# The second attention layer's latent projections as seven block products, with other places for modulation passes, squares and weight sums

## The chip, the core and the metric

The kernel runs on one core of a Trainium2 chip. The core's engines are TensorE (PE; its weight loads are PEld), VectorE (DVE), ScalarE (ACT), GpSimd (POOL) and SyncE (SP), with 16 DMA engines. SBUF is the memory beside the engines, PSUM the banks that matrix products write. The metric is the device time of one execution in microseconds (us); 2938.09 is the median of three.

## The reference

All data are float32, the width D is 1024, and there are 512 latent and 256 context tokens. The time looked at here is the first of two blocks, two layers of attention:

```python
hx = rmsnorm(x, norm_w) * (1 + scale) + shift       # latent, 512 tokens
hc = rmsnorm(cx, norm_w) * (1 + scale_c) + shift_c  # context, 256 tokens
px, pc = split_cols(hx @ w_in), split_cols(hc @ w_in)   # q, k, v of A, B, C and gates
ya = global_gqa(...)           # A: 8 heads, 2 of k and v, q and k normed, rope
yb = neighbourhood_attn(...)   # B: 8 heads, relative bias, masked by place
yc = window_gqa(...)           # C: 8 heads, 2 of k and v, rope, band mask, sink
x = x + gate * (concat(ya, yb, yc) * silu(px[9])) @ w_out
```

In layer 0 the context's outputs are needed too, in layer 1 the latent ones alone. Modulation vectors of the second block (`silu(c) @ w_mod`), which need nothing of the attention, are also computed meanwhile. The second block (an RG-LRU and Hyena layer and a conformer, each with a mixture of experts) is not touched.

## The kernel before

**Pairs and steps.** Heads are worked in 12 pairs, `PAIRS`: four B, four A, four C. A pair has one step for each tile of 128 queries: 6 in layer 0 (768 tokens), 4 in layer 1 (512). `schedule` (L272) writes one order of items for a layer, and each engine's `attention` walks through it: `S` (scores of both heads into BIG, L1402 to L1413), `T` (transposes of the step before's probabilities, L1426, into PT, which ACT copies at L2156), `E` (exponentials, ACT L2145), a filler, and `O` (outputs, PE L1442, read by DVE at L2613). DVE adds biases (L2707) or masks (L2718), takes the maximum (L2723), and after the exponentials scales by the reciprocal sum (L2604, L2606). The `T` of a step stands behind the `S` of the next.

**Projections.** The filler of a pair's steps is the next pair's projections: one unit of weights (1024 x 256) for keys and values (`kv`; one for each B pair, one for all A, one for all C) and one for queries and gates (`qg`, each pair). In layer 0 they go by blocks: the unit and the tokens are cut into 2 x 2 blocks, and `BLOCK_PRODUCTS`, seven products in the order 1, 2, 6, 5, 7, 3, 4, take the place of eight, each of `BLOCK_K` = 4 matmuls of 128 x 128 by 384 tokens into one of the two PJ banks (L1097 is the helper that issues every matmul). ACT copies products 1, 6, 5 and 4 out of PSUM (L2091), DVE adds 2, 7 and 3 to them (L2560). For it DVE makes four sums of token blocks once (`block_tokens`, into `BLOCK_TOKENS` in XC) and POOL four sums of weight blocks a unit (`add_weights`, L1031 to L1036), one of them in place in the weight ring W. `block_slots` (L168) deals the items out over the steps by `weight`.

In layer 1 each of k, v, q and g is a plain product (`through`: 8 matmuls over K of 512 latent columns, and of 256 context columns for k and v). A and C pairs get their values by token tiles (`vt`: 48 matmuls of 128 columns, copied by DVE, `values` L2694). Then come, in A pairs, the `norm_` items (squares by ACT L2177, L2178, sums by PE L1354, ACT L2125, L2129), in A and C pairs the `rope_` items (PE L1364, DVE L2584 to L2588). In B pairs and in layer 0 `v_tokens` (L1345) transposes the values. Gates go through a tanh (ACT L2102) and a product on DVE.

**Modulation.** 168 passes over rows of 1024 weights on DVE (L2462, each with a read of its accumulator) stand in the order as `mod` items. `plan_modulation` (L90) gives each step a room (`MODS_ROOM`), none in C heads and none in the last step but one from the last B pair on; `schedule` puts the first 1 (layer 0's B heads) or 2 of a step ahead of `E`, and `with_modulation` the others between fillers. POOL loads the rows into a ring of five places (`mod_place`, L1001): the next load waits for the passes of the row five before.

**POOL's queue** is one list, sorted by place in the order: row loads, biases (L991), weight sums, reloads. The sums of a unit wait for product 3 (the sixth) of the unit before. Behind the list POOL reloads the context (L1064, after h was scaled) and two weights of the second block (L1066, L1067).

Of the kernel before, what the change touches and what calls it, by code (L numbers as in the profile page):

```python
# [17 lines left out]
P = 128  # L18
# [68 lines left out]
MODS_ROOM = [{"B": 3.6, "A": 1.4, "C": 0.0}, {"B": 2.6, "A": 2.6, "C": 0.0}]  # L87


def plan_modulation():  # L90


    out, room = [], 0.0
    pause = 0
    for layer in range(DEPTH):
        tiles = STEPS[layer] // len(PAIRS)
        for n in range(STEPS[layer]):
            i, t = divmod(n, tiles)
            at = n + (STEPS[0] if layer else 0)
            ropes = t == tiles - 2 and i >= 3  # L100
            room += 0.0 if ropes else MODS_ROOM[layer][PAIRS[i][0]]
# [8 lines left out]
    assert all(at < 8 * 6 or STEPS[0] <= at < STEPS[0] + 8 * TT for at in out)  # L110
    return out


MOD_STEPS = plan_modulation()
MODS_SECOND = MOD_STEPS[MODS_FIRST - 1] + 1

# [19 lines left out]
BLOCK_N = NA // 2  # L136
# [7 lines left out]
def inserted_by_blocks(i):  # L144
# [6 lines left out]
    elif kind == "B":  # L151
        out += by_blocks(i, "kv")
    elif kind == "A" and j == 0:
        out += by_blocks(i, "kv", 0, 6) + [("square", i, "k")] + by_blocks(i, "kv", 6) + [("norm_k", i)]
    elif j == 0:
        out += by_blocks(i, "kv")
# [11 lines left out]
def block_slots(i, tiles):  # L168


    todo = inserted_by_blocks(i)
    early = BLOCK_K if PAIRS[i - 1][0] != "B" else 0
    room = tiles if PAIRS[i][0] == "B" else tiles - 1
    total, done, least, before = sum(weight(x) for x in todo[early:]), 0, 0, 0
    out = [(-1, item) for item in todo[:early]]
    for item in todo[early:]:
        at = max(min(int(done * room / total), room - 1), least)
        done += weight(item)
# [8 lines left out]
def inserted(layer, i):  # L187


    if layer == 0:  # L190
        return inserted_by_blocks(i)
    kind, j = PAIRS[i]
    parts = 2 if layer == 0 else 1

    def through(what, parts):
        return [("mm", i, what, part, k) for part in range(parts) for k in range(KT)]

    def by_tokens(tiles):
        return [("vt", i, t, k) for t in tiles for k in range(KT)]

    if kind == "B":
        out = through("k", 2) + through("q", parts) + through("v", 2)
        gates = through("g", parts)
        return out + gates[:BLOCK_K] + [("v_tokens", i)] + gates[BLOCK_K:]
    if j == 0:
        out = through("k", 2) + through("q", parts)
        if kind == "A":
            out.append(("norm_k", i))
        out += by_tokens(range(4)) + by_tokens(range(4, 6))
        if kind == "A":  # L210
            out.append(("norm_q", i))
        return out + [("rope_k", i)] + through("g", parts) + [("rope_q", i)]
    gates = through("g", parts)
    out = through("q", parts)
    if kind == "C":
        return out + [("rope_q", i)] + gates
    if parts == 2:
        return out + gates[:KT] + [("norm_q", i)] + gates[KT:] + [("rope_q", i)]
    return out + [("norm_q", i)] + gates + [("rope_q", i)]


def weight(item):
# [4 lines left out]
    return {"block": 1.5, "square": 0, "tanh": 0, "gate": 0, "next": 0, "vt": 0.5, "v_tokens": 2.5, "norm_k": 3, "norm_q": 3, "rope_k": 2, "rope_q": 2}[what]  # L227
# [9 lines left out]
def filler(item):  # L237
# [3 lines left out]
    return item[0] == "vt" or item[0] == "block" and item[4] < BLOCK_K - 1  # L241


def begins_unit(item):

    if item[0] == "mm":
        return item[2] in ("k", "q") and item[3:] == (0, 0)
# [24 lines left out]
def schedule(layer):  # L272
# [6 lines left out]
    for i in range(1, len(PAIRS)):  # L279
        if layer == 0:  # L280
            for at, item in block_slots(i, tiles):
                slots[(i - 1) * tiles - 1 + at].append(item)
            continue
        todo = inserted(layer, i)
        total, done, least, before = sum(weight(x) for x in todo), 0, 0, None
        for item in todo:
            at = min(int(done * tiles / total), tiles - 1)
            done += weight(item)
            if item[0].startswith(("norm_", "rope_")):

                least = min(at + (before is not None and before >= at), tiles - 1)
            at = max(at, least)
            before = at
            slots[(i - 1) * tiles - 1 + at].append(item)
    tail = 1 + max(n for n in slots if any(item[0] in ("mm", "vt", "block") for item in slots[n]))
# [5 lines left out]
    for n in range(-1, last + 1):  # L301
        if n + 1 <= last:
            order.append(("S", n + 1))
        if n >= 0:
# [3 lines left out]
            early = 1 if layer == 0 and steps[n][0] < 4 else 2  # L308
# [116 lines left out]
def build(nc, A):  # L425
# [15 lines left out]
    with ExitStack() as ctx:  # L441
# [79 lines left out]
        def mod_place(row):  # L521

            x = row % MOD_RING
# [117 lines left out]
        def sem(name):  # L641
# [103 lines left out]
        BLOCK_TOKENS = XC[:, :, :].rearrange("p a b -> p (a b)")\  # L745
            .rearrange("p (x k n) -> p x k n", x=4, n=BLOCK_N)
        ADDED = ARENA_AND_RS[:, ROPE_AT + N:ROPE_AT + N + 3 * BLOCK_K * P]\
            .rearrange("p (x k n) -> p x k n", x=3, n=P)

        def block_uses():  # L750
# [3 lines left out]
            for y, item in enumerate(schedule(0)[1]):  # L754
# [10 lines left out]
                elif what.startswith("norm_"):  # L765
                    me.next_pj()
                    me.next_pj()
# [4 lines left out]
        def block_parts(i, which, dst, src, half):  # L772


            a = half * BLOCK_N
            if PAIRS[i][0] != "B" or which == "g":
                return [(dst[:, a:a + BLOCK_N], src[:, 0:BLOCK_N])]
            rows = BLOCK_N // GRID_W
            grid = dst[:, 0:N].rearrange("p (c r) -> p c r", r=ROWS)
            if half == 0:  # L780
                return [(grid[:, :, 0:rows], by_columns(src[:, 0:BLOCK_N]))]
            n = N - BLOCK_N
            return [(grid[:, :, rows:ROWS], by_columns(src[:, 0:n])), (dst[:, N:NA], src[:, n:BLOCK_N])]
# [97 lines left out]
        def row_place(x):  # L881
# [3 lines left out]
            freed = -1 if x < MOD_RING else max(place["mod", y] for y, (row, _) in enumerate(MOD_OPS) if row == x - MOD_RING)  # L885
            second = x % MOD_RING >= 2 and min(steps) >= STEPS[0]
# [97 lines left out]
        def _(pool):  # L984
# [9 lines left out]
            def load_mod_rows(x):  # L994


                if x >= MOD_RING:
                    pool.wait_ge(mod_made, ROW_DONE[x - MOD_RING])
                if row_place(x)[1]:
                    pool.wait_ge(products_filled, len(LATE))  # L1000
                pool.dma_start(mod_place(x), A["mod_rows"][x]).then_inc(mod_loaded[x % MOD_RING], 16)  # L1001
# [12 lines left out]
            first_block_unit = first_units.index(("w_in", 0, 1))  # L1014

            def weights_of(u):

                n = first_block_unit + u
# [3 lines left out]
            def add_weights(u):  # L1022
# [4 lines left out]
                if u:  # L1027
                    pool.wait_ge(pj_filled, uses[u - 1][5][0])
                else:
                    pool.wait_ge(h_scaled, 2 * KT)  # L1030
# [3 lines left out]
                pool.tensor_tensor(a21, a21, a11, ALU.add).then_inc(weights_added, 1)  # L1034
# [12 lines left out]
            for u in range(len(uses)):  # L1047
                jobs.append((uses[u - 1][5][1] if u else -1, 3, u))
            jobs.append((uses[-1][6][1], 4, 0))
            for _, what, x in sorted(jobs):  # L1050
                if what == 3:
                    add_weights(x)
                elif what == 4:
                    pool.wait_ge(pj_filled, uses[-1][6][0])
# [8 lines left out]
            pool.wait_ge(h_scaled, 4 * KT)  # L1063
# [2294 lines left out]
```

## Time and profile before

| | us |
|---|---|
| median of the runs (2937.65 to 2938.37) | 2938.09 |
| the profiled execution | 2939.53 |
| its span | 2937.7 |
| PE busy in the span | 2817.2 (96%) |
| DVE busy | 1363.4 (46%) |
| ACT busy | 770.1 (26%) |
| POOL busy | 225.2 (8%) |

Layer 0's attention takes the span's 44 to 669 us (B heads to 339, A heads to 536), its output products follow to 771, and layer 1's attention runs from 779 to 1289 (B heads to 1020, A heads to 1186, C heads to 1289; the filler, which is one pair ahead, changes its kind about one pair earlier). The rest, to 2938, is the second block. A busy share over the whole span says little of a stage; the windows and waits below do.

### The profile page before, as it was taken

To read this page: it belongs to the slowest core of one execution; us is meant where nothing else is said; L and a number is where in the kernel's file an instruction comes from. 1 tells how busy PE (TensorE), PEld (TensorE's weight loads), DVE (VectorE), ACT (ScalarE), POOL (GpSimd) and SP (SyncE) were. 2 spreads that over 40 slices of the span, in tenths; PEclk is the share of its full clock that TensorE was granted. 3 is DMA by queue.
4 is the path that set the end of the run, shared out by engine and by line. 5 is a ranking of instruction groups with operands and counts; after the bars stand their busy time and mean duration, and the time that the engine had idled before them with its cause. 6 is when DMAs were issued, how large, how long until landed. Compare 5 with 4: busy or idle time off the path is not lost.

```text
span 2937.7 us, 33851 instructions
## 1 busy us (share of the span) xinstructions
PE 2817.2 (96%) x13312; PEld 1523.4 (52%) x13312; DVE 1363.4 (46%) x2569; ACT 770.1 (26%) x1410; POOL 225.2 (8%) x253
## 2 busy tenths in 40 slices
PE   7999899999999999999999989999999999999998
PEld 3555555655555655576444644444445734444442
DVE  2696776775355674674485741111115813121112
ACT  3334454441222453433251120000003232000001
POOL 2233212100011010000000000000002300000000
PEclk9999999999999999999999999999999999999999
DMA  8244222111145443112110158999993217999996
GB/s 315 90 162 153 91 73 87 37 73 58 79 155 169 135 152 106 44 46 89 63 61 20 56 216 359 421 421 422 421 420 145 107 67 299 410 421 422 421 421 282
DMA packets 90673, 586.60 MB, mean 200 GB/s; under 512 B 10192, under 2 KB 10192, under 8 KB 29232
## 3 DMA queue, kind: packets, MB, share of 16 engines
q1 hardware_dynamic: 69696, 502.56, 42.6%
q0 software_dynamic: 20848, 82.26, 8.4%
q8 instruction: 89, 1.46, 0.2%
q14 instruction: 40, 0.33, 0.0%
HBM read 582.68 MB, written 2.10 MB: 199 GB/s over the span
## 4 chain that ended last, share of the span: by engine, by line
PE 68%; DVE 6%; ACT 2%; issue 1%; DVEq 0%; ACTq 0%
PE BIG L1097 43%; PE PJ L1097 11%; PE BIG L1941 4%; PE PT L1426 2%; PE PT L1442 2%; DVE ARENA L2984 1%; PE PT L1097 1%; PE BIG L1409 1%; PE PJ L1146 1%; PE BIG L1413 1%; PE PT L1917 1%; DVE ARENA L3036 0%; DVE ARENA L3035 0%; ACT ARENA L2145 0%; PE BIG L1402 0%
## 5 line engine op out<-in xcount | busy, mean ns | idle before, releaser
L1097 PE MATMUL BIG<-ARENA 128*64 128x512 f32 (+3 forms) x2720 | 565.4, 458 | 6.5 <-DVE ARENA L3058 2.5
L1097 PEld LDWEIGHTS BIG<-ARENA 128*64 128x64 f32 (+1 forms) x2720 | 302.2, 169 | 255.4 <-issue 224.3
L1097 PE MATMUL PJ<-HT,W 128*128 128x512 f32 (+2 forms) x1040 | 400.3, 533 | 7.3 <-DVE ARENA L2694 2.6
L1097 PE MATMUL BIG<-W,ARENA 128*64 128x512 f32 (+1 forms) x1280 | 282.0, 573 | 0.9 <-DVE ARENA L2906 0.9
L1097 PEld LDWEIGHTS PJ<-HT,W 128*128 128x128 f32 x1040 | 193.8, 193 | 166.3 <-issue 127.9
L3087 DVE SCALAR_TENSOR_TENSOR XC<-BIG,MOD,XC 128x512 f32<-128x512 f32 x128 | 90.2, 747 | 379.4 <-PE BIG L1941 379.4
L2156 ACT ACTIVATE ARENA<-PT 128x512 f32<-128x512 f32 (+1 forms) x264 | 145.1, 583 | 416.8 <-PE PT L1426 416.5
L1097 PE MATMUL BIG<-HT,W 128*128 128x512 f32 (+1 forms) x600 | 236.6, 553 | 2.4 <-DVE ARENA L2860 2.1
L1097 PEld LDWEIGHTS BIG<-W,ARENA 128*64 128x64 f32 (+1 forms) x1280 | 107.4, 142 | 161.0 <-issue 154.9
L2723 DVE TENSOR_REDUCE STAT<-BIG 128x1 f32<-128x512 f32 (+5 forms) x240 | 169.9, 724 | 39.2 <-PE BIG L1413 34.2
L1097 PE MATMUL BIG<-HT,ARENA 128*64 128x512 f32 (+1 forms) x632 | 182.9, 573 | 0.0
L1097 PEld LDWEIGHTS BIG<-HT,W 128*128 128x128 f32 x600 | 114.3, 191 | 120.5 <-issue 111.7
L2145 ACT ACTIVATE ARENA<-BIG,STAT 128x512 f32<-128x512 f32 (+5 forms) x240 | 170.6, 717 | 22.3 <-DVE STAT L2723 21.3
L1426 PE MATMUL PT<-CONST,ARENA 128*128 128x128 f32 x1024 | 150.7, 282 | 22.0 <-DVE ARENA L2613 14.5
L1426 PEld LDWEIGHTS PT<-CONST,ARENA 128*128 128x128 f32 x1024 | 111.5, 141 | 82.8 <-issue 60.8
L1442 PEld LDWEIGHTS PT<-ARENA 128*64 128x64 f32 x2048 | 110.3, 136 | 68.9 <-issue 63.9
L2462 DVE CUSTOM_DVE_ANT_0 SPILL<-ARENA,W,VEC 128x1024 bf16<-128x1024 f32 x100 | 139.1, 1391 | 4.3
L1442 PE MATMUL PT<-ARENA 128*64 128x128 f32 x2048 | 139.3, 278 | 1.4 <-ACT ARENA L2156 1.4
L1097 PE MATMUL BIG<-ARENA,W 128*128 128x512 f32 (+2 forms) x400 | 136.2, 494 | 0.1
L2606 DVE TENSOR_SCALAR ARENA<-ARENA,STAT 128x512 f32<-128x512 f32 (+3 forms) x240 | 128.3, 535 | 8.5
L1941 PE MATMUL BIG<-ARENA 128*128 128x512 f32 x256 | 115.0, 602 | 0.0
L3077 DVE TENSOR_TENSOR ARENA<-ARENA,BIG 128x1024 f32<-128x1024 f32 x16 | 19.5, 1221 | 204.2 <-PE BIG L1097 204.2
(325 smaller groups left out, 3068.4 us busy)
## 6 DMA issues: line engine op xcount, KB each, us to landing
ARENA<-in_exp_w SPq DMA_DIRECT2D x168, 1024.0 KB, 18.1
W<-in_exp_w SPq DMA_DIRECT2D x144, 1024.0 KB, 16.7
W<-in_units SPq DMA_DIRECT2D x89, 1024.0 KB, 4.9
HT<-in_exp_w SPq DMA_DIRECT2D x72, 1024.0 KB, 21.9
ARENA<-in_mod_rows POOLq DMA_DIRECT2D x76, 512.0 KB, 4.5
W<-in_mod_rows POOLq DMA_DIRECT2D x52, 512.0 KB, 4.5
ARENA<-in_bias_b POOLq DMA_DIRECT2D x16, 384.0 KB, 4.9
XC<-in_x SPq DMA_DIRECT2D x1, 3072.0 KB, 10.1
```

Source lines behind the costliest of these rows:

```text
L1097: ins = pe.matmul(out, lhsT, rhs, start=start, stop=stop, skip_group_check=skip)
L1146: last = pe.matmul(PJ[0][:, 0:512], const("ident"), CONST[:, 0:512], start=True, stop=True)
L1409: pe.matmul(BIG[h][:, N - (b - a) * P:N], Q[rows, i % 2, t * P:t * P + P], keys[rows, a * P:b * P], start=True, stop=True)
L1426: last = pe.transpose(PT[:, a:a + P], PROB[:, h, y * P:y * P + P], const("ident"))
L1442: last = pe.matmul(PT[head * HD:head * HD + HD, bank * 512:bank * 512 + P], V[:, buf_of[i], tile, head * HD:head * HD + HD], PTS[:, at:at ...
L1941: last = pe.matmul(BIG[k_use % 2][:, half * N:half * N + N], YK[:, m * P:m * P + P], GSCAT[:, :], start=True, stop=True)
L2145: act.activation(PROB[:, h, 0:b - a], BIG[h][:, a:b], ACT.Exp, bias=STAT[:, c:c + 1], accum_out=STAT[:, 4 + c:5 + c]).then_inc(probs_exp, 1)
L2156: act.activation(PTS[:, a:a + w], PT[:, bank:bank + w], ACT.Copy).then_inc(t_copied, 1)
L2462: dve.tensor_tensor_reduce(SPILL[:, :], mod_place(row), MODV[:, which, :], 1.0, vec("mod_b", at), ALU.mult, ALU.add, MOD[:, at:at + 1]).th ...
L2606: dve.tensor_scalar(probs, probs, STAT[:, 8 + c:9 + c], None, ALU.mult)\
L2723: dve.tensor_reduce(STAT[:, c:c + 1], out[:, a:b], AX.X, ALU.max, negate=True).then_inc(max_ready, 1)
L3087: ins = dve.scalar_tensor_tensor(XC[:, m, 0:N], BIG[k_use % 2][:, half * N:half * N + N], mod(group, 5, m, 0), XC[:, m, 0:N], ALU.mult, AL ...
```

## The change

- In layer 1 the latent part of `qg` of all pairs and of `kv` of all but the first pair goes by blocks too: 7 products of 4 matmuls by 256 columns. Context columns of k and v stay plain products. `vt` and `values` go; A and C values are transposed by `v_tokens`. DVE makes four token sums at the start of the layer, in parts of XC and U that hold nothing else then; POOL sums weights for 17 more units, one sum now in `THIRD_SUMS` in Q beside the latent columns.
- `block_slots` deals out both layers: a `square` goes one step behind the item before it (at most to the last step of the room), a `norm_` not before it; ropes stand in the last step of the filler, ahead of the first block product of the pair behind it (before, in A pairs, behind the last gate columns, in C pairs behind the queries).
- `modulation_room` gives the passes: 62, 27 and 17 in layer 0's B, A and C heads (before 71, 27 and 0), and 62 in layer 1, 12 of them in its C heads (before 70 and none). One pass of a step (before two, in layer 1) stands ahead of `E` in B heads. Rows whose passes lie in C heads use only two places of the ring (`plan_row_places`).
- `ADDED_AHEAD` sorts a unit's weight sums 16 items earlier in POOL's list.
- The reload of the context waits for layer 1's last block product.

```diff
-MODS_ROOM = [{"B": 3.6, "A": 1.4, "C": 0.0}, {"B": 2.6, "A": 2.6, "C": 0.0}]
+MODS_ROOM = [{"B": 2.9, "A": 1.4, "C": 0.7}, {"B": 2.3, "A": 1.4, "C": 0.8}]
+MODS_ROOM_OF = {("B", 0): 1.8, ("B", 1): 3.0, ("B", 2): 2.6, ("B", 3): 3.2, ("B", 4): 3.8, ("B", 5): 3.0}
+MODS_NONE = [(0, 3, 4), (0, 4, 0), (1, 3, 2), (1, 4, 0)]
+def modulation_room(layer, i, t):
+    kind = PAIRS[i][0]
+    if layer == 0 and (kind, t) in MODS_ROOM_OF:
+        return MODS_ROOM_OF[kind, t]
+    if t == STEPS[layer] // len(PAIRS) - 2 and kind == "A" or (layer, i, t) in MODS_NONE:
+        return 0.0
+    return MODS_ROOM[layer][kind]
...
+def plan_row_places():
...
+        at = min(range(2 if outputs else MOD_RING), key=lambda x: (last_of[x], x))
...
-BLOCK_N = NA // 2
+BLOCK_TOKENS_OF = [NA, N]
+BLOCK_NS = [n // 2 for n in BLOCK_TOKENS_OF]
...
+    elif kind == "B" or j == 0:
         out += by_blocks(i, "kv")
+        if layer:
+            context = [[("mm", i, what, 1, k) for k in range(KT)] for what in ("k", "v")]
+            squares = [("square", i, "k")] if kind == "A" else []
+            out += context[0] + squares + context[1] + ([("norm_k", i)] if kind == "A" else [])
...
+        if item[0] == "square":
+            squared = min(before + 1, room - 1)
+            out.append((squared, item))
+            continue
+        if item[0].startswith("norm_"):
+            at = least = max(at, squared)
...
-            early = 1 if layer == 0 and steps[n][0] < 4 else 2
+            early = 1 if steps[n][0] < 4 else 2
...
+        def third_sum(w, layer, k):
+            return THIRD_SUMS[:, k // 2, k % 2, :] if layer else w[:, k, P:2 * P]
...
+            ADDED_AHEAD = 16
...
-                jobs.append((uses[u - 1][5][1] if u else -1, 3, u))
+                jobs.append((uses[u - 1][5][1] - ADDED_AHEAD if u % BLOCK_UNITS else layer_starts[u // BLOCK_UNITS] - 1, 3, u))
...
-            pool.wait_ge(h_scaled, 4 * KT)
+            pool.wait_ge(pj_filled, uses[-1][6][0])
             pool.dma_start(XC[:, :, N:NA], A["ctx2"]).then_inc(ctx2_loaded, 16)
...
-            def block_tokens():
+            def block_tokens(layer):
+                dve.wait_ge(h_ready, (3 if layer else 2) * KT)
...
+                n = BLOCK_NS[layer]
```

## Rows read from the trace of the kernel before

**Rows 1.** Windows of five stretches: start:end, length, busy PE, PEld, DVE, ACT, POOL; clock.

```profile
44.00:300.00 256.00, 243.12 (x1174) 147.88 (x1174) 194.09 (x369) 95.77 (x212) 85.43 (x90) 0.98 0.44 150
300.00:669.00 369.00, 348.89 (x2137) 214.95 (x2138) 261.79 (x595) 173.66 (x378) 56.48 (x56) 0.99 0.21 68
779.00:979.00 200.00, 200.00 (x910) 115.60 (x910) 101.85 (x210) 60.44 (x135) 20.99 (x39) 1.00 0.43 147
979.00:1186.00 207.00, 193.72 (x1218) 120.22 (x1216) 130.87 (x243) 87.70 (x165) 17.21 (x31) 0.99 0.37 123
1186.00:1289.00 103.00, 100.86 (x675) 62.52 (x674) 75.08 (x200) 48.15 (x107) 0.00 (x0) 1.00 0.09 31
```

**Rows 2.** Waits of PE, 44 to 669 us: total us, times, longest.

```profile
PE PT L1426 <- DVE ARENA L2613: 14.5, 11, 3.2
PE PT L1426 <- ACT ARENA L2156: 6.1, 12, 1.3
```

**Rows 3.** Waits of PE, 779 to 1230 us.

```profile
PE BIG L1409 <- DVE ARENA L2588: 7.9, 5, 1.8
```

**Rows 4.** Windows of 10 us with a low clock, columns as in group 1.

```profile
115.00:125.00 10.00, 7.54 (x32) 4.97 (x29) 9.68 (x18) 3.95 (x9) 3.91 (x5) 0.83 0.81 267
1162.00:1172.00 10.00, 7.44 (x14) 2.98 (x13) 3.79 (x8) 1.97 (x5) 0.00 (x0) 0.83 0.32 105
```

**Rows 5.** Chain of work, 779 to 1230 us: start, us, what.

```profile
779.72 30.94 PE PJ L1097 x88
811.43 3.44 PE PJ L1097 x8
...
984.18 10.98 PE PJ L1097 x96
```

**Rows 6.** Timeline of DVE, 784 to 816 us: start, us, what, idle before.

```profile
815.53 0.69 DVE L2536 SCALAR_TENSOR_TENSOR ARENA<-ARENA,PJ 128x512 f32<-128x512 f32 x1 [29.62 <-ACT ARENA L2052]
```

**Rows 7.** Timelines of PE, DVE and ACT, a B step of layer 1.

```profile
872.75 0.70 PE L1402 MATMUL BIG<-ARENA 64*128 64x256 f32 x4
...
874.75 9.19 PE L1097 MATMUL PJ<-HT,W 128*128 128x256 f32 x24
...
873.92 0.43 DVE L2707 TENSOR_TENSOR BIG<-BIG,ARENA 128x256 f32<-128x256 f32 x1 [0.67 <-PE BIG L1413]
...
876.06 1.27 DVE L2462 CUSTOM_DVE_ANT_0 SPILL<-ARENA,W,VEC 128x1024 bf16<-128x1024 f32 x1
...
879.48 0.49 DVE L2606 TENSOR_SCALAR ARENA<-ARENA,STAT 128x512 f32<-128x512 f32 x1
...
876.76 0.19 ACT L2145 ACTIVATION_READ_ACCUMULATOR ARENA<-BIG,STAT 128x1 f32 x1
```

**Rows 8.** Timelines of PE and ACT, an A step of layer 1.

```profile
1054.82 1.13 PE L1409 MATMUL BIG<-ARENA 64*128 64x512 f32 x4
...
1058.10 0.60 PE L1426 MATMUL PT<-CONST,ARENA 128*128 128x128 f32 x4
...
1060.89 0.21 ACT L2145 ACTIVATION_READ_ACCUMULATOR ARENA<-BIG,STAT 128x1 f32 x1
```

**Rows 9.** Window of one C pair of layer 1, columns as in group 1.

```profile
1214.50:1242.90 28.40, 28.40 (x176) 16.42 (x174) 19.38 (x53) 12.31 (x28) 0.00 (x0) 1.00 0.12 38
```

**Rows 10.** Instructions of line 2462: min/median/max ns, first and last start.

```profile
L2462 DVE DVE_READ_ACCUMULATOR2_ANT MOD<- x168: 75/83/86, 99.5 to 1148.6; 128x1 f32 x168
L2462 DVE CUSTOM_DVE_ANT_0 SPILL<-ARENA,W,VEC x100: 1274/1280/2171, 112.0 to 1147.4; 128x1024 bf16<-128x1024 f32 x100
```

**Rows 11.** Groups of POOL, 44 to 700 us: busy us, mean ns, idle before.

```profile
L1034 POOL TENSOR_TENSOR W<-W 128x512 f32<-128x512 f32 x17 | 29.3, 1721 | 0.0
...
L1031 POOL TENSOR_TENSOR ARENA<-W 128x512 f32<-128x512 f32 x17 | 22.7, 1334 | 133.9 <-PE PJ L1097 130.6 <-DVE HT L2488 3.2
```

**Rows 12.** Timelines of DVE and PE, layer 0, 230 to 235 us.

```profile
230.29 2.06 DVE L2462 CUSTOM_DVE_ANT_0 SPILL<-ARENA,W,VEC 128x1024 bf16<-128x1024 f32 x1
...
234.81 0.63 PE L1426 MATMUL PT<-CONST,ARENA 128*128 128x128 f32 x4 [2.45 <-DVE ARENA L2613]
```

More of the change, by code:

```diff
@@ L109, in plan_modulation @@
     assert len(out) == len(MOD_OPS) and out[MODS_DONE[1] - 1] < STEPS[0]
-    assert all(at < 8 * 6 or STEPS[0] <= at < STEPS[0] + 8 * TT for at in out)
     return out
 MOD_STEPS = plan_modulation()
+def plan_row_places():
+    last_of = [-1] * MOD_RING
+    places, before, uses = [], [], [0] * MOD_RING
+    counts = []
+    for row in range(len(MOD_ROWS)):
+        steps = [MOD_STEPS[y] for y, (x, _) in enumerate(MOD_OPS) if x == row]
+        outputs = any(8 * 6 <= at < STEPS[0] or at >= STEPS[0] + 8 * TT for at in steps)
+        at = min(range(2 if outputs else MOD_RING), key=lambda x: (last_of[x], x))
+        places.append(at)
+        before.append(last_of[at])
+        last_of[at] = row
+        uses[at] += 1
+        counts.append(uses[at])
+    return places, before, counts
+ROW_PLACE, ROW_BEFORE, ROW_COUNT = plan_row_places()
 MODS_SECOND = MOD_STEPS[MODS_FIRST - 1] + 1
@@ L165, in inserted_by_blocks, with block_slots @@
     return out + ropes + [("tanh", i), ("next", i), ("gate", i)]
-def block_slots(i, tiles):
-    todo = inserted_by_blocks(i)
+def block_slots(layer, i):
+    tiles = STEPS[layer] // len(PAIRS)
+    todo = inserted(layer, i)
     early = BLOCK_K if PAIRS[i - 1][0] != "B" else 0
     room = tiles if PAIRS[i][0] == "B" else tiles - 1
-    total, done, least, before = sum(weight(x) for x in todo[early:]), 0, 0, 0
+    squared, total, done, least, before = 0, sum(weight(layer, x) for x in todo[early:]), 0, 0, 0
     out = [(-1, item) for item in todo[:early]]
@@ L177, in block_slots @@
         at = max(min(int(done * room / total), room - 1), least)
-        done += weight(item)
+        done += weight(layer, item)
         if item[0] == "next":
@@ L184, in block_slots, with weight @@
     return out
[L187 to L222, printed above, removed]
+def weight(layer, item):
     what = item[0]
@@ L226, in weight @@
         return 2 if item[3] == 0 else 1
-    return {"block": 1.5, "square": 0, "tanh": 0, "gate": 0, "next": 0, "vt": 0.5, "v_tokens": 2.5, "norm_k": 3, "norm_q": 3, "rope_k": 2, "rope_q": 2}[what]
+    return {"block": BLOCK_NS[layer] / 256, "square": 0, "tanh": 0, "gate": 0, "next": 0, "v_tokens": 2.5, "norm_k": 3, "norm_q": 3, "rope_k": 2, "rope_q": 2}[what]
 def late_transposes(layer, i, t):
@@ L279, in schedule @@
     for i in range(1, len(PAIRS)):
[L280 to L293, printed above, removed]
+        for at, item in block_slots(layer, i):
             slots[(i - 1) * tiles - 1 + at].append(item)
-    tail = 1 + max(n for n in slots if any(item[0] in ("mm", "vt", "block") for item in slots[n]))
+    tail = 1 + max(n for n in slots if any(item[0] in ("mm", "block") for item in slots[n]))
     for y, item in enumerate(first_products()):
@@ L765, in block_uses @@
                 elif what.startswith("norm_"):
-                    me.next_pj()
-                    me.next_pj()
+                    for _ in range(1 if what == "norm_q" and layer else 2):
+                        me.next_pj()
                 elif what.startswith("rope_"):
@@ L2089, in attention @@
                         scale = -1.0 if tile else block_scale(i, which)
-                        for out, src in block_parts(i, of, dst, PJ[use[0]], half):
+                        for out, src in block_parts(layer, i, of, dst, PJ[use[0]], half):
                             ins = act.activation(out, src, ACT.Copy, scale=scale)
@@ L2558, in attention @@
                         scale = -1.0 if tile else block_scale(i, which)
-                        for out, src in block_parts(i, of, dst, PJ[use[0]], half):
+                        for out, src in block_parts(layer, i, of, dst, PJ[use[0]], half):
                             ins = dve.scalar_tensor_tensor(out, src, scale, out, ALU.mult, ALU.add)
```

210 lines of the change are left out of this document (86 added, 124 removed).

## The prediction

> **What bounds the kernel now.** I read the stretches first, then the waits of TensorE (PE), then single steps. The five stretches [rows 1] are the two attention layers, by kind of head: layer 0's masked B heads, its A and C heads together, then B, A and C of layer 1. PE is the bound: it is busy 200.00 of 200 us in layer 1's B heads, and in the other four leaves 12.9, 20.1, 13.3 and 2.1 us idle, 33.0 us in layer 0 and 15.4 in layer 1. VectorE (DVE) is next: 194.09 of 256 us in layer 0's B heads, 75.08 of 103 in layer 1's C heads. The idle time of layer 0 is mostly PE waiting for DVE to read an output (L2613) and for ScalarE (ACT) to copy transposed probabilities (L2156) [rows 2]; that of layer 1 is mostly the end of a rope, L2588 [rows 3]. After long waits PE's granted clock falls to the lower of its two levels (1.2 for 2.4 GHz) for a moment: four 10 us stretches show 0.83, three of them in layer 0 (first and last stand there), 1.7 us lost in each [rows 4]. Everything behind layer 1 waits for PE's progress, so what is won there arrives at the end.
>
> **PE work of layer 1 (sure).** In the chain [rows 5] 8 records of 512 columns take 3.44 us, 0.430 each, and two records are one matmul. The 88 records from 779.72 are 56 of these and 32 of 256 columns: (30.94 - 56 x 0.430) / 32 = 0.214 us. A latent projection of two column tiles is now 32 records of 512, 13.76 us; as 7 products of 4 matmuls it is 56 of 256, 12.01 us. That saves 1.75 us in each of 15 units (12 for queries and gates, 3 for keys and values of B heads): 26.2 us. For the two A and C key units it is 6.88 + 3.43 (keys) + 10.98 (values by token tile, the 96 records of 984.18) = 21.29 us before, and 12.01 + 32 x 0.214 (context) + 6 transposes of 128 columns at 10.98/96 = 0.114, so 19.5 after: 3.5 us for both. **Sum -29.8 us.** Beside it and free: four token sums on DVE, before the first block product; DVE is idle for 29.62 us up to 815.53 [rows 6], and PE is busy with pair 0's keys and values, which no block enters, for the first 20 us of that. The context reload moves behind the last block product on GpSimd's (POOL's) queue, with the two weight loads behind it; what uses them stands behind the last heads and the output products.
>
> **Old waits of layer 1.** Behind a pair's ropes, in the same step, now stands the next pair's first block product, 8 x 0.214 = 1.72 us of PE work against 7.9 / 5 = 1.6 for each wait [rows 3], and the token-tile products go with the wait for their copy. If nothing came in their place the 13.3 us of A heads and 1.7 us of clock would return: **-15.0 us**.
>
> **New waits of layer 1 (the doubtful term).** Seven products share two banks: each must be read by ACT (products 1, 6, 5, 4) or DVE (2, 7, 3) before the next but one may use its bank. A product of layer 0 gives 8 records of 384 columns as cover, 2.6 us by the mean of the two prices above, one of layer 1 only 1.72, and with 4 instead of 6 steps to a pair 1.75 to 2.5 products stand in a step. Both readers serve the next step's softmax first. In a B step [rows 7] PE starts its fill 2.0 us after the scores began, ACT is free at 4.2, DVE has its maxima at 3.3, ends the two passes at 6.0 and the probabilities at 7.2; with one pass ahead of them, as the change has it, at 7.2 - 1.36 = 5.9. So in the step in which the keys' fifth product ends, the seventh could start at 4.2 but waits until DVE has read a bank, 5.9 + 0.43 (a sum of 128x256 there) = 6.3: 2.1 us; an estimated half microsecond comes in each of the two steps behind, as DVE is late there: 3 us in each of three pairs, 9. In an A step [rows 8] transposes end 3.9 us after the scores began and ACT's exponentials at 6.3. The fourth product waits 1.3 us for DVE, the sixth 0.7 for ACT's copy of the fourth, and the moved square stands behind the exponentials, so its sums wait 1.5: 3.5 us in three pairs, 10.5. By the same hand tally the first A pair with its norm of keys comes to 4, the first C pair with two ropes to 3.7. In a C pair DVE has 19.38 us of work to 28.4 of PE [rows 9]; it gets three block sums of 0.43 and three modulation passes (1.28 and an accumulator read of 0.08 [rows 10]) on top: 24.8, against 28.4 - 1.75 = 26.6 us of PE work left, 1.8 us of slack, and the rope falls into one step. I put the wait of the first C pair, 3.7 us, on each of three pairs and 2 on the last, which has no projection beside it: 13. That is 40 us, each wait counted alone; a wait shortens those behind it, and I take four fifths: **+32 us**. Ends: 16, if the engines make good half of a step's lag in the next, and 48, if the POOL sums stretch DVE's work as in layer 0.
>
> **POOL sums.** The 17 new units issue four sums of 1.33 to 1.72 us, about 6.0 us a unit [rows 11]; they begin when the sixth product of the unit before is done, and PE has its last product (1.72) and the next two (3.4) ahead of the first use: 5 us, in which two sums, at most 3.1 us, are needed. So only their effect on DVE counts. A pass beside them takes 2.06 us instead of 1.28, and PE waits 2.45 us for the output queued behind it [rows 12]. The Trainium skill (SBUF — State Buffer, Who interferes with whom) says that such a DVE operation and a GpSimd operation hold a shared port pair exclusively, so that the later one is blocked for the whole of the other. The row fits a pass that waited for the rest of a sum, not one that waited for a whole one; by the rule to its end see the last rival. Sorting the sums 16 program items earlier only puts them ahead of row loads that wait for DVE: nothing in the sum, since PE waits for no POOL sum now.
>
> **Layer 0.** The passes go from 71, 27 and 0 (B, A, C heads) to 62, 27 and 17, by the planner's arithmetic; those beside POOL sums fall from 4 to 3 a step. Of the waits for L2613 (14.5 us, 11 times [rows 2]) the longest ones should lose one pass each: with the clock -8 us. The later squares free ACT's copies (up to 1.3 us a pair [rows 2]), but the sums now wait for the square: -2. In C heads a pass lies mostly where DVE waits for ACT; rope steps and the last pair, which has no fill, pay: +5. **-5 us**, ends -12 (no charge in C) and +3 (no gain in B).
>
> **Sum.** -29.8 - 15.0 + 32 - 5 = -17.8 us. The profiled execution took 2939.53 us (span 2937.7), the median of the runs is 2938.09; taken off the median: **2920 us**.
>
> **Rivals.**
> *The waits overlap.* At the lower end of the new waits: -29.8 - 15 + 16 - 5 = -33.8, 2904 us. For it: in layer 0, products with the same two banks cost PE little; against it: there a step has one and a half products.
> *The banks eat it.* All 40 us and nothing won in layer 0: -4.8, 2933 us, no change. For it: ACT and DVE end every step's softmax after PE could go on [rows 7, 8].
> *Slower: DVE becomes the bound of the C heads.* From the point where a C pair's DVE work reaches PE's 26.6 us (24.8 plus what sums stretch), each of the 29 passes in C heads costs its full 1.36 us: 39.4 in place of the 5 and, of the 13 at four fifths, 10.4 charged above. -17.8 + 24.0 = +6.2, 2944 us. For it: 75.08 of 103 us already. Against it: DVE waits for ACT in each of these steps, and a pass put there is half hidden.
> *The sums shut DVE out.* If each new sum blocked DVE for its whole length, the three units in C heads, where DVE has no slack, would add 3 x 6.0 [rows 11]: about flat, 2938 us. For it: passes beside sums do get longer. Against it: the pass of 2.06 us [rows 12] is only 0.78 longer than alone, half of a sum. That is the rule of the Trainium skill (SBUF — State Buffer, Who interferes with whom) taken to its end.
>
> **How the numbers follow.** Forecast 0.50 (2908 to 2932 by itself), overlapping waits 0.22, eaten gain 0.14, slower 0.09, shut out 0.05. The range runs from 2897 (both low ends: -29.8 - 15 + 16 - 12 = -40.8) to 2941; what is left out is most of the slower case and the ends beyond. A change under 0.2%, 5.9 us, can't be told from none. Faster: nearly all of the first two, 0.70; within: most of the eaten gain, the shut-out and the forecast's upper edge, 0.19; slower 0.11.
>
> **What would show it.** Right: PE records of 256 columns in place of 512 with layer 1 some 15 us shorter; in B heads one wait of about 2 us a pair for L2560's successor (DVE, block sums); in A heads waits for ACT's copies and squares; C heads no shorter than before. Layer 0: fewer and shorter waits for L2613 in B heads. Wrong: layer 1 shorter by 25 us or more with PE busy throughout (the waits overlap), C pairs of 30 us (DVE the bound), or waits of PE for POOL's sums, which I left out.

## The result and the profile after

The changed kernel takes 2946.91 us (median of nine, 2943.92 to 2948.37) where the kernel before takes 2938.09 (2937.22 to 2940.63): ratio 1.0028, interval 1.0019 to 1.0037. **It is 8.8 us slower by the medians; 18 us faster were forecast.** The profiled execution took 2943.92 us, the lowest of the nine, with a span of 2942.1, so the traces explain 4.4 us of span. The other 4.4 have no trace: the profiled execution before was 1.4 us above its median, this one is 3.0 below its own.

In the table, a stage ends with the end of the DVE row that reads its last output (L2613 before, L2588 after); "B heads" of layer 1 begins with its first output. Idle is the sum of PE's pauses over 0.15 us from 779 us to the end of layer 1, with their number. The kernels e4 to e15 are told of below.

| us | before | after | e4 | e6 | e5 | e9 | e15 |
|---|---|---|---|---|---|---|---|
| layer 0, last output at | 671.6 | 667.6 | 669.1 | 667.5 | 668.2 | 669.4 | 665.3 |
| layer 1, B heads | 182.1 | 186.9 | 180.3 | 186.3 | 184.3 | 184.3 | 185.7 |
| A heads | 166.3 | 161.1 | 161.1 | 161.4 | 160.2 | 154.6 | 153.1 |
| C heads | 102.7 | 108.4 | 106.9 | 101.0 | 103.2 | 101.0 | 101.0 |
| the three together | 451.1 | 456.4 | 448.3 | 448.7 | 447.7 | 439.9 | 439.8 |
| PE idle (pauses) | 15.1 (13) | 40.2 (46) | 32.7 (43) | 33.7 (36) | 10.5 (25) | 10.6 (22) | 10.2 (21) |
| from there to the end | 1648.9 | 1650.8 | 1652.5 | 1651.5 | 1649.3 | 1656.6 | 1652.6 |

The same stretches as in [rows 1], after (busy PE, PEld, DVE, ACT, POOL; granted clock, DMA share, GB/s):

```profile
44.00:300.00 256.00, 249.41 (x1211) 151.46 (x1211) 185.42 (x357) 95.26 (x214) 86.02 (x85) 0.99 0.41 143
300.00:669.00 369.00, 344.99 (x2118) 212.12 (x2117) 276.38 (x619) 175.50 (x377) 57.96 (x64) 1.00 0.24 78
779.00:979.00 200.00, 188.32 (x1096) 153.06 (x1095) 117.91 (x223) 59.92 (x146) 73.81 (x73) 0.99 0.37 132
979.00:1186.00 207.00, 189.56 (x1278) 141.25 (x1277) 124.49 (x240) 100.78 (x196) 37.46 (x42) 0.99 0.26 86
1186.00:1289.00 103.00, 91.82 (x689) 67.73 (x689) 87.06 (x222) 48.40 (x112) 18.43 (x21) 1.00 0.29 96
```

In layer 0's B heads PE's idle time fell from 12.9 to 6.6 us. Layer 1's B heads, where PE never paused, now show 11.7 us of idle time, and its C heads 11.2 for 2.1. Who ended the waits there, 779 to 1291 us (total us, times, longest):

```profile
PE PJ L1113 <- DVE ARENA L2535: 16.5, 10, 3.3
PE PJ L1359 <- ACT ARENA L2163: 6.5, 4, 2.8
PE PT L1431 <- DVE ARENA L2588: 4.7, 9, 1.3
PE PJ L1113 <- ACT ARENA L2083: 4.5, 7, 1.3
...
PE BIG L1414 <- DVE ARENA L2563: 1.5, 3, 0.6
```

L2535 is DVE's block sum and L2083 ACT's block copy, the two readers of a bank; L2163 is the square ahead of a norm. L2563 is the end of a rope, whose waits fell from 7.9 us [rows 3] to 1.5. One B step, the answer to [rows 7], timelines of PE, then DVE, then POOL:

```profile
870.61 1.89 PE L1113 MATMUL PJ<-HT,ARENA 128*128 128x256 f32 x8
875.81 2.98 PE L1113 MATMUL PJ<-ARENA,W 128*128 128x256 f32 x8 [3.31 <-DVE ARENA L2535]
...
871.49 1.28 DVE L2448 CUSTOM_DVE_ANT_0 SPILL<-W,VEC 128x1024 bf16<-128x1024 f32 x1
...
872.88 1.31 DVE L2581 TENSOR_SCALAR ARENA<-ARENA,STAT 128x512 f32<-128x512 f32 x1
...
874.30 1.12 DVE L2581 TENSOR_SCALAR ARENA<-ARENA,STAT 128x512 f32<-128x512 f32 x1
875.35 0.74 DVE L2535 SCALAR_TENSOR_TENSOR ARENA<-PJ,ARENA 128x256 f32<-128x256 f32 x2
...
872.66 1.26 POOL L1046 TENSOR_TENSOR ARENA<-W 128x512 f32<-128x512 f32 x1 [6.66 <-PE PJ L1113]
873.99 1.15 POOL L1048 TENSOR_TENSOR ARENA<-ARENA,W 128x512 f32<-128x512 f32 x1
```

The last product, number 4, may start when DVE has read number 7 out of the bank that both use. DVE ends its maxima, one pass, and then the two scalings of probabilities, which take 1.31 and 1.12 us, where [rows 7] has 0.49: POOL's weight sums for the next unit began at 872.66, when the product before was done. The 8 records behind the wait then take 2.98 us (1.99 in the same place of e4, below), as the granted clock is at its lower level for 3.4 us. Two windows of 10 us in layer 1 show that, each with 1.7 us lost:

```profile
870.00:880.00 10.00, 6.69 (x26) 5.29 (x24) 7.54 (x13) 2.77 (x7) 6.89 (x6) 0.83 0.07 13
980.00:990.00 10.00, 7.16 (x38) 4.57 (x33) 5.41 (x12) 6.46 (x11) 0.67 (x2) 0.83 0.48 161
```

### The profile page after: what moved, and what is told of

It is laid out like the page before. It is cut to its first block, busy times and chain, and to the rows that moved or that the text cites. A ratio compares the mean times of both kernels' runs of the same rounds, so it can differ in the third digit from the quotient of the medians.

```text
span 2942.1 us, 34737 instructions
## 1 busy us (share of the span) xinstructions
PE 2797.8 (95%) x13604; PEld 1589.9 (54%) x13604; DVE 1393.7 (47%) x2620; ACT 788.9 (27%) x1464; POOL 317.8 (11%) x321
## 4 chain that ended last, share of the span: by engine, by line
PE 64%; DVE 9%; ACT 2%; issue 2%; DVEq 0%; ACTq 0%
PE BIG L1113 43%; PE PJ L1113 8%; PE BIG L1944 4%; PE PT L1445 1%; DVE ARENA L2952 1%; PE PT L1431 1%; PE PT L1113 1%; PE PJ L1162 1%; DVE SPILL L2448 1%; PE BIG L1414 1%; ACT ARENA L2131 1%; DVE STAT L2691 1%; PE PT L1920 1%; PE BIG L1418 1%; DVE ARENA L2581 1%
## 5 line engine op out<-in xcount | busy, mean ns | idle before, releaser
L1113 PE MATMUL PJ<-HT,W 128*128 128x256 f32 (+2 forms) x832 | 239.4, 438 | 4.3 <-ACT HT L2031 2.4
L1113 PEld LDWEIGHTS PJ<-HT,W 128*128 128x128 f32 x832 | 155.9, 193 | 68.7 <-issue 27.9
L1113 PE MATMUL PJ<-XC,ARENA 128*128 128x384 f32 (+1 forms) x544 | 161.0, 435 | 11.1 <-DVE ARENA L2535 8.9
L1431 PE MATMUL PT<-CONST,ARENA 128*128 128x128 f32 x1024 | 152.3, 281 | 20.0 <-DVE ARENA L2588 12.8
L2581 DVE TENSOR_SCALAR ARENA<-ARENA,STAT 128x512 f32<-128x512 f32 (+3 forms) x240 | 136.2, 568 | 8.5
L1113 PEld LDWEIGHTS PJ<-XC,ARENA 128*128 128x128 f32 x544 | 99.2, 190 | 51.8 <-DVE ARENA L2535 13.4
L2448 DVE CUSTOM_DVE_ANT_0 SPILL<-W,VEC 128x1024 bf16<-128x1024 f32 x85 | 117.5, 1382 | 3.2 <-DMA W<-in_mod_rows 1.7
## 6 DMA issues: line engine op xcount, KB each, us to landing
XC<-in_x SPq DMA_DIRECT2D x1, 3072.0 KB, 10.1
```

The source lines that it names most:

```text
L1113: ins = pe.matmul(out, lhsT, rhs, start=start, stop=stop, skip_group_check=skip)
L1431: last = pe.transpose(PT[:, a:a + P], PROB[:, h, y * P:y * P + P], const("ident"))
L2448: dve.tensor_tensor_reduce(SPILL[:, :], mod_place(row), MODV[:, which, :], 1.0, vec("mod_b", at), ALU.mult, ALU.add, MOD[:, at:at + 1]).th ...
L2581: dve.tensor_scalar(probs, probs, STAT[:, 8 + c:9 + c], None, ALU.mult)\
```

## The experiments

Ratios are to the kernel before, with their intervals; times are medians. Where a kernel mixes block and plain products, the plain ones are the eight matmuls of 512 columns of before.

**e1: layer 0 alone.** The kernel before with this, and with the change's ring places for rows:

```diff
-MODS_ROOM = [{"B": 3.6, "A": 1.4, "C": 0.0}, {"B": 2.6, "A": 2.6, "C": 0.0}]
+MODS_ROOM = [{"B": 2.9, "A": 1.4, "C": 0.7}, {"B": 2.6, "A": 2.6, "C": 0.0}]
+MODS_ROOM_OF = {("B", 0): 1.8, ("B", 1): 3.0, ("B", 2): 2.6, ("B", 3): 3.2, ("B", 4): 3.8, ("B", 5): 3.0}
...
+        if item[0] == "square":
+            squared = min(before + 1, room - 1)
...
-                jobs.append((uses[u - 1][5][1] if u else -1, 3, u))
+                jobs.append((uses[u - 1][5][1] - 16 if u else -1, 3, u))
```

> The kernel before with the change's layer 0 alone: its places for modulation passes (17 of them in C heads), squares one step later, weight sums 16 items ahead; layer 1 keeps plain products and has its 62 passes in B and A heads. Theory (the loss is in layer 1's block products: seven short products through two banks wait for their readers, and each stop of PE costs more than its idle time): layer 0's attention ends some 4 us earlier and the whole is faster by about 4 us, 2934. Rival (passes in masked C heads are what costs): no gain, 2938 or more, with C heads of layer 0 longer by 4 us than before. Rival (weight sums hold VectorE): as the theory.

2938.9 us, ratio 1.0002 (0.9992 to 1.0012). In the trace layer 0's last output comes at 668.9, 2.7 us earlier than before, and the span is 2.2 us shorter, but the medians don't differ. This is the first rival's side, with its sign: layer 0's C heads take 139.7 us, 4.2 longer than before; with A heads, 4.8 longer, they pay back most of the 11.6 us that B heads win. So layer 0 is not where the loss is, and its gain is 0 to 3 us, not the 5 forecast.

**e2 and e3: blocks in a part of layer 1's heads.** The changed kernel, in which `PLAIN` names what stays plain in layer 1 (e2: A and C heads; e3: B heads):

```diff
+def plain(layer, i, which):
+    return layer == 1 and (PAIRS[i][0], which) in PLAIN
...
+    if plain(layer, i, "qg"):
+        queries, gates = [[("mm", i, what, 0, k) for k in range(KT)] for what in ("q", "g")]
...
+        return out + queries[:BLOCK_K] + values + queries[BLOCK_K:] + [("square", i, "q")] + gates + [("norm_q", i), ("next", i)] + ropes + [("tanh", i), ("next", i), ("gate", i)]
```

> The changed kernel with plain products for A and C heads of layer 1, blocks for B heads alone. Theory: the seven B units save 12.3 us of matmuls and pay some 13 us of waits, 2 us of clock and 2 of stops, so this half brings a few us of loss; with layer 0's gain 2936 to 2940. Rival (C heads' passes): the passes stay, so 2942 or more. Rival (sums): seven units of sums instead of 17, 4 us of the loss left, 2940.

> The changed kernel with plain products for B heads of layer 1, blocks for A and C heads alone. Theory: ten units save 17.5 us and pay some 27 us of waits and 5 of stops where 15 stood before; about even with plain products, 2934 to 2940. Rival (C heads' passes): 2942 or more. Rival (sums): 2941.

2941.79 us, 1.0008 (0.9998 to 1.0018), and 2942.13, 1.0011 (1.0001 to 1.002): each about a third of the loss. Both lie above the theory's ranges, next to what the rivals said (2942 or more, and 2940 or 2941), so these two runs don't choose between the causes. By pairs of the same kind in the traces: B1 takes 47.7 us plain (before and e3) and 50.4 by blocks; A1 35.5 before, 36.0 by blocks, 34.4 plain in the new order (e2); C1 28.4 before, 29.9 by blocks, 29.8 plain with the new passes.

**e4: no weight sums beside DVE.** The changed kernel with, in layer 1, sums of one column:

```diff
+                n = 1 if layer else P
-                pool.tensor_tensor(ADDED[:, 0], a21, a22, ALU.add).then_inc(weights_added, 1)
+                pool.tensor_tensor(ADDED[:, 0, :, 0:n], a21[:, :, 0:n], a22[:, :, 0:n], ALU.add).then_inc(weights_added, 1)
```

> The changed kernel with layer 1's weight sums cut to one column of each block (the other columns are left out), so that GpSimd works next to nothing beside VectorE. Theory: the wait of a B pair for the sum of its seventh product falls from 3.3 to about 1.9 us, as the probabilities no longer take 1.31 and 1.12 us, and passes get shorter; 4 to 8 us faster than the changed kernel, 2939 to 2943. Rival (sums hold VectorE, and this is the whole loss): 2930 or less. Rival (C heads' passes): within 3 us of the changed kernel.

2935.81 us, 0.9992 (0.9982 to 1.0002): 11 us less than the changed kernel's median, more than the theory's 4 to 8. Its trace shows layer 1 8.1 us shorter, 6.6 of them in B heads. The same B step, PE and DVE:

```profile
873.50 1.99 PE L1114 MATMUL PJ<-ARENA,W 128*128 128x256 f32 x8 [1.85 <-DVE ARENA L2536]
...
872.03 0.49 DVE L2582 TENSOR_SCALAR ARENA<-ARENA,STAT 128x512 f32<-128x512 f32 x1
...
872.63 0.49 DVE L2582 TENSOR_SCALAR ARENA<-ARENA,STAT 128x512 f32<-128x512 f32 x1
873.03 0.75 DVE L2536 SCALAR_TENSOR_TENSOR ARENA<-PJ,ARENA 128x256 f32<-128x256 f32 x2
```

The probabilities take 0.49 us again and the wait is 1.85 us for 3.31. But 32.7 us of idle time are left.

**e5: the new order without blocks.** All of layer 1 plain, passes in its B and A heads as before.

> The changed kernel with plain products in the whole of layer 1, but in the change's new order (ropes ahead of the next pair's first matmuls, squares a step later, values transposed), and with layer 1's passes in B and A heads alone, as before. Theory (the blocks themselves lose in layer 1, by the waits for their readers and the sums beside VectorE, while the order of ropes and squares wins): A pairs of 34 to 35 us where 35.5 stood, B and C heads as before, layer 1 some 4 us shorter than before; with layer 0's 2.7 the whole is 2931 to 2935. Rival (the blocks win and only C heads' passes lose): no faster than layer 0 alone, 2936 to 2939.

2935.18 us, 0.9989 (0.998 to 0.9998): at the theory's upper edge. The gain over e1 is in the A heads, 160.2 us for e1's 165.6: the next pair's first matmuls stand behind the ropes, and the waits of [rows 3] don't come back.

**e6 and e8: no passes in layer 1's C heads,** alone (e6) and with e4's sums (e8):

```diff
-MODS_ROOM = [{"B": 2.9, "A": 1.4, "C": 0.7}, {"B": 2.3, "A": 1.4, "C": 0.8}]
+MODS_ROOM = [{"B": 2.9, "A": 1.4, "C": 0.7}, {"B": 2.6, "A": 2.6, "C": 0.0}]
...
+    if layer == 1:
+        return 0.0 if t == STEPS[layer] // len(PAIRS) - 2 and i >= 3 else MODS_ROOM[layer][kind]
```

> The changed kernel with layer 1's passes placed as before, none in its C heads. Theory: C heads come from 108.4 to some 105 us, A heads and B heads, which take the 12 passes, lose 1 to 3; 0 to 3 us faster than the changed kernel, 2943 to 2946. Rival (C heads' passes are the loss): 6 us or more faster than the changed kernel, 2940 or less.

> The small weight sums of e4 (all columns but one of each block left out) together with passes as before in layer 1. Theory: the two causes stand beside each other: e4's 2935 less 1 to 3 us, 2932 to 2935; the rest of the forecast gain is still missing, as the waits of the two banks stay. Rival (the sums and the passes in C heads are the whole loss): 2925 or less.

e6: 2939.98 us, 1.0006 (0.9997 to 1.0015), 7 us less than the changed kernel, which is on the rival's side: C heads fell by 7.4 us, and the B and A heads that took the 12 passes lost nothing. e8: 2931.64 us, 0.9979 (0.9968 to 0.9989). The two effects nearly add up (15 us together, 11 and 7 alone), and what is left of the change brings 7 us, not 18; e5 has about half of that without any block. Waits of C heads, after (1183 to 1291 us):

```profile
PE PT L1431 <- DVE ARENA L2588: 3.0, 6, 1.3
PE BIG L1414 <- ACT ARENA L2131: 2.2, 3, 1.1
PE PJ L1113 <- DVE ARENA L2535: 1.6, 2, 0.8
```

and in e6 (1182 to 1284 us):

```profile
PE BIG L1416 <- ACT ARENA L2133: 1.8, 3, 0.9
PE PJ L1115 <- ACT ARENA L2085: 1.5, 3, 0.5
...
PE PT L1433 <- DVE ARENA L2590: 0.3, 1, 0.3
```

**e7: sums later.** In layer 1 the sums wait until DVE has scaled the probabilities of the step behind the sixth product:

```diff
+                if later(u):
+                    pool.wait_ge(probs_scaled, 2 * (STEPS[0] + scaled_after(u)[1] + 1))
```

> The changed kernel, in which the weight sums of layer 1 wait until VectorE has scaled the probabilities of the step that follows the sixth product (not those of keys' units behind a B pair, which would come too late). Theory: the probabilities of these steps take 0.49 again, but the passes and block sums behind them now meet the sums; a part of what the small sums brought, 1 to 4 us faster than the changed kernel, 2942 to 2946. Rival (any sum beside VectorE costs the same, wherever it lies): within 1 us of the changed kernel. Rival (TensorE waits for the sums): slower than it.

2952.75 us, 1.0051 (1.0036 to 1.0067): slower, the last rival. PE waited three times, 2.2 us together, for a weight sum, and 18.8 us for block sums where 16.5 stood:

```profile
PE PJ L1127 <- DVE ARENA L2549: 18.8, 10, 3.2
...
PE PJ L1127 <- POOL ARENA L1059: 2.2, 3, 1.3
```

The weight sums now met other operations of DVE: 16 passes took 1.81 us on the mean, and three of the products behind a norm 1.30 to 1.75 instead of 0.75. The block sums themselves kept their 0.42 us; they came later. Moving the meeting to this place doesn't help; only taking it away did.

**e11: stores for sums.** POOL fills the places of layer 1's sums instead of adding:

```diff
+                if layer:
+                    pool.memset(ADDED[:, 0], 0.0).then_inc(weights_added, 1)
...
+                    return
                 pool.tensor_tensor(ADDED[:, 0], a21, a22, ALU.add).then_inc(weights_added, 1)
```

> The changed kernel in which GpSimd fills the places of layer 1's weight sums with zeros instead of adding (the sums are left out): it waits and writes at the same points, but reads nothing. Theory (sums cost by GpSimd and VectorE working on the same memory at once, not by the length of GpSimd's queue): if fills take the same path as sums, probabilities beside them still stretch and the time is that of the changed kernel, 2943 to 2947; if reading is what matters, as with the small sums, 2935 to 2938. Rival (the queue, and weights that come late): as the changed kernel if the fills are as long as the sums.

2942.14 us, 1.0008 (0.9998 to 1.0017), between the two ranges. A fill takes 0.53 to 0.57 us on the mean, a sum in the changed kernel 1.30 to 1.55. By the rows that overlap POOL's in layer 1, passes beside fills take 1.28 us on the mean of 11, as alone, those beside sums in the changed kernel 1.61 on the mean of 14; probabilities 0.64 beside fills, 1.11 beside sums, 0.49 alone (six each). The longest wait of a block sum is 2.3 us. That is nearly e4; but the granted clock cost 6.8 us in layer 1 here (four times 3.4 us at the lower level), 1.7 in e4. Why it fell more often is open. This loss differs between executions of kernels with blocks in all heads: 1.7 us in e8, 3.4 in the changed kernel and e6, 5.1 in e7 and e12, 8.5 in e13, which is the changed kernel but for the place of its sums.

**e12: short reads.** ACT and DVE read one column of each block product in layer 1:

```diff
+                            if layer:
+                                out, src = out[:, 0:1], src[:, 0:1]
                             ins = act.activation(out, src, ACT.Copy, scale=scale)
```

> The changed kernel in which, in layer 1, ScalarE and VectorE read one column of each block product in place of 256 (the rest of queries, keys, values and gates of that layer is left out). Theory (TensorE waits because the readers are busy with the next step's softmax and come late, not because they read long): the 3.3 us waits of B pairs lose some 0.4 to 0.7, those of A and C pairs 0.2 to 0.4; 5 to 9 us faster in all. Rival (the length of the reads is the wait): the waits for block sums and copies, 16.5 and 4.5 us, fall under 6 together.

2941.79 us, 1.0005 (0.9996 to 1.0015), 5 us less than the changed kernel: the lower end of the theory. Idle time falls from 40.2 to 35.8 us, and the two readers' waits are still there:

```profile
PE PJ L1113 <- DVE ARENA L2539: 13.9, 10, 3.1
...
PE PJ L1113 <- ACT ARENA L2085: 3.0, 7, 1.1
```

The readers come late, behind the next step's softmax; it isn't the reading that is long.

**e9, e10, e15: blocks in C heads only.** e9 is e5 with blocks in layer 1's C heads; e10 has layer 0's passes as before too; e15 is e9 with layer 0's room in C heads at 0 and layer 1's at 3.8 (B) and 2.0 (A):

```diff
-MODS_ROOM = [{"B": 2.9, "A": 1.4, "C": 0.7}, {"B": 2.6, "A": 2.6, "C": 0.0}]
+MODS_ROOM = [{"B": 2.9, "A": 1.4, "C": 0.0}, {"B": 3.8, "A": 2.0, "C": 0.0}]
```

> The changed kernel with plain products for B and A heads of layer 1, blocks for its C heads alone, and its passes in B and A heads as before. Theory (without passes beside them the blocks of C heads bring about 2 us, in B and A heads plain products in the new order are better): some 2 us below the plain version, 2932 to 2935, and the fastest whole kernel of the study. Rival (blocks lose in every kind of head): 2936 or more.

> As e9, with layer 0's passes as before too (71, 27 and none in C heads). Theory: layer 0's new places bring 3 us of the profiled time, so 2 to 4 us slower than e9. Rival (layer 0's gain of 11 us in B heads is paid back in A and C heads): within 1.5 us of e9.

> e9 with the 17 passes of layer 0's C heads moved to layer 1's B and A heads (B from 39 to 57, A from 23 to 22), where TensorE is busy throughout and VectorE is not. Theory (passes in C heads cost about a quarter of a microsecond each, those beside plain B heads nothing): layer 0's C heads 3 to 4 us shorter, layer 1's B heads the same, 2927 to 2930. Rival (layer 1's B heads then wait for VectorE as layer 0's did): no faster than e9, 2931 or more.

e9: 2931.0 us, 0.9971 (0.9959 to 0.9983), a little better than its theory. With e5 and e6, which have the same passes, it tells the kinds of heads apart. Against e5, which has no blocks, layer 1 is 7.8 us shorter in the traces (4.2 in the medians): in C heads the five units of blocks bring most of the 8.8 us that their price promises (5 x 1.75). Against e6, which has blocks in all heads, it is 8.8 us shorter (9.0 in the medians): in B and A heads the blocks lose.

e10: 2941.56, 1.001 (1.0001 to 1.0019), but not for the reason that it was to test: in layer 0's B heads stands one new wait of PE for a copy of ACT,

```profile
PE PJ L1140 <- ACT ARENA L2121: 9.7, 3, 9.2
```

and behind it on ACT and POOL:

```profile
267.82 1.91 ACT L2188 ACTIVATE W<-W 128x2048 f32<-128x2048 f32 x1 [8.30 <-DMA W<-in_mod_vectors]
...
259.61 0.53 POOL L1045 DMA_DIRECT2D W<-in_mod_vectors  x1
```

The load of the modulation vectors stands behind weight sums that were sorted ahead of it; in the trace of the kernel before, it was issued 10.7 us earlier:

```profile
248.95 0.53 POOL L1007 DMA_DIRECT2D W<-in_mod_vectors  x1
```

So e10 says nothing of the rooms. By this timeline it shows what the earlier place of the sums can cost; no run has these rooms with the sums at their former place.

e15: **2925.67 us, 0.996 (0.9946 to 0.9974), the fastest kernel of the study, ahead of the kernels before and after.** Each of its five times lies below each of e9's six, and the median below its theory's range. Layer 0's C heads end 4.1 us earlier than in e9, 1.3 of it by the granted clock, and layer 1's B heads, which take 18 more passes, still leave PE no pause. e9, then e15, in layer 1's B heads:

```profile
836.00:971.00 135.00, 135.00 (x671) 79.91 (x671) 77.69 (x160) 39.69 (x92) 18.08 (x34) 1.00 0.52 175
```

```profile
831.00:967.00 136.00, 136.00 (x677) 80.60 (x679) 93.64 (x185) 39.72 (x92) 24.76 (x46) 1.00 0.65 224
```

**e13 and e14: sums not ahead.** `ADDED_AHEAD = 0` in the changed kernel (e13) and in e9 (e14).

> The changed kernel with the weight sums at their former place in GpSimd's queue (no items ahead). Theory of the prediction: nothing, within 1.5 us of the changed kernel, 2945 to 2949. Rival (the earlier place makes row loads late): 3 us or more faster, 2944 or less. Rival (the earlier place lets sums start in time, as row loads that wait for VectorE stood ahead of them): slower by 2 us or more, with TensorE waiting for GpSimd's sums.

> e9 with the weight sums at their former place in GpSimd's queue. Theory: within 1.5 us of e9, 2930 to 2933. Rivals as for e13, on the same sides.

2947.59 us, 1.0029 (1.0018 to 1.004), and 2929.87, 0.9968 (0.9956 to 0.998): no clear difference from the changed kernel and from e9, as the theory.

## Why the prediction was wrong

Against the forecast sum of -17.8 us the spans differ by +4.4, 22.2 us apart. From layer 0's last output to layer 1's, -12.8 was forecast and +6.5 came: 19.3 us. The terms, in the prediction's order:

- **PE work, -29.8: right but for its price.** Block records follow each other at 4.32/20 = 0.216 us, not 0.214, and the token-tile records of before did so at 0.112, not 0.114: about 2 us. That weights are now loaded for every 256 columns instead of 512 (PEld busy 153.06 of 200 us for 115.60 in B heads) is not a bound: 0.216 is half of the 0.430 of 512 columns.
- **Old waits, -15.0: right for the waits that it names.** The waits for the token tiles' copy went, and those for ropes fell to 1.5 us. The order by itself does not bring 15 us: in e5, without blocks, it has 10.5 us of pauses in other places, and layer 1 is 3.4 us shorter than before.
- **New waits, +32: the step that failed,** in three ways. (1) Idle time rose by 25.1 us, where -13.3 and +32 make 18.7: 6.4 more. Without sums beside DVE it rose by 17.6 (e4), so the waits for late readers were, in sum, sized right: **the POOL sums were put only into the upper end,** though the row of the stretched pass was at hand [rows 12]; in the B step they stretch the probabilities, which were taken at 0.49. (2) **A pause costs more than its idle time.** A record of 256 columns is shown with 0.382 us, and the next one in a row starts 0.216 after it. Behind a pause there is no such overlap, so each pause loses an estimated 0.166 us that the profile shows as busy:

```profile
L1113 PE MATMUL PJ<-XC,ARENA 128*128 128x256 f32 x272 | 65.6, 382 | 8.5 <-DVE ARENA L2535 7.2 <-ACT ARENA L2083 1.3
```

```profile
886.93 4.32 PE PJ L1113 x20
```

  The first row is a group (count, busy, mean ns), the second a piece of the chain. 46 pauses in place of 13 are 5.5 us, which no term held. (3) After long waits the granted clock fell to its lower level twice in this execution; the sum had taken even the one time of before as won: 3.4 us. With the 2 above these make 17.3 of the 19.3 us; the other 2 stay open.
- **POOL sums, "only their effect on DVE counts": right in words, wrong in size.** PE waits for no sum. Their effect is 7.5 us of pauses and 8.1 us of layer 1 (e4), 11 us in the medians. The Trainium skill (SBUF — State Buffer, Who interferes with whom) says that a DVE operation that needs the port pair shared with GpSimd is blocked for the whole of a GpSimd operation that came first. The traces agree in direction: probabilities and passes stretch beside sums, and passes don't beside fills, which read nothing (e11). In size they show at most 0.8 us more for probabilities, less than one sum. The rival of the shut-out (6 us for each unit in C heads) named the wrong place: C heads lost 1.5 us by the sums, B heads 6.6.
- **Passes in C heads.** The term for them, 13 us of waits and +5 in layer 0, had the right size: layer 1's C heads wait 11.0 us (13 at four fifths is 10.4), and layer 0's C heads take 4.4 us more. Without the passes layer 1's C heads win 7.4 us (e6) and layer 0 ends 4.1 earlier (e15). What was missed is that the passes have a free place: in plain B heads they cost nothing (e15).
- **Earlier place of the sums, nothing:** right in this kernel (e13) and in e9 (e14), with some luck: with other rooms PE waits 9.2 us behind it (e10).
- **Layer 0, -5:** in the trace its last output comes 4.0 us earlier: B heads 10.1 us shorter, A heads 1.6 and C heads 4.4 longer. Waits for the output fell from 14.5 to 8.1 us [rows 2], while the sums of norms, put at 2 us of gain, now wait 4.6 us for squares. The counts of passes were off: the kernel before has 74, 27 and 0 in layer 0's heads and 67 in layer 1, not 71 and 70. And the gain in the trace is no more than clock: the lower level cost layer 0 7.9 us before and 3.3 after, but 3.2 to 7.0 in the twelve traces with the change's layer 0, which ended at 667.5 to 670.7. The medians of e1 show no gain; behind layer 1, where these kernels do the same work, the traces lose another 15.5 to 23.9 us to the lower clock, and that spread is more than the gain.

Outside the stretch of the 19.3 us the rest of the 22.2 is 1.0 us in layer 0 and 1.9 behind layer 1, 1.7 of it clock.

The slower rival, 2944 us, came nearest, but not as told: its sign, C pairs of 30 us, came (31.5 and 29.9), but DVE is not the bound of the C heads (87.06 of 103 us busy), each of the 12 passes there costs 0.6 of its 1.36 us (e6), and the sums took the other part of the loss. The 4.4 us of the medians that the traces don't hold stay open. The granted clock of layer 1, which cost 1.7 to 8.5 us in the traces of such kernels, could hold a part of them; that is not shown.

## What to carry to other kernels

Fewer multiplications by shorter products pay only while every bank's readers come in time: here they won 7.8 us in C heads without passes and lost 8.8 in B and A heads. Count pauses as well as idle microseconds, and charge each the difference between a lone record and one in a row. Price helper work on a second engine by what it does to the first one's operations on the same memory, not by its own waits. Work that fits anywhere belongs beside the engine that never pauses: 17 passes moved from masked heads to plain ones brought 4 to 5 us, where the whole change lost 9.

## What the runs showed of the hardware

- Probabilities (128x512, one input) take 0.49 us alone, 1.11 on the mean beside POOL's sums, 0.64 beside POOL's fills; passes 1.28, 1.61 and 1.28.
- DVE's block sums (128x256, one input in PSUM) keep their 0.42 us beside POOL's sums.
- A record of 256 columns is shown with 0.382 us; in a row the next one starts 0.216 after it.
- How often the granted clock falls in layer 1 is not settled: once to five times 3.4 us at the lower level in traces of kernels with blocks in all heads.
